# Short MLP of a two-sequence encoder layer: weights loaded raw and split on GpSimd, in place of split copies made in the long down stage

## The reference

```python
def encoder_layer(x, ...):
    ...                                    # RG-LRU branch and attention branch, merged
    x = layer_norm(ALPHA * x + mix, ln1_g, ln1_b)
    hu = depthwise_conv(x @ w_up + b_up, w_ffn_conv, b_ffn_conv, FFN_CONV_PAD)   # w_up: 1024 x 6144
    val, gt = jnp.split(hu, 2, axis=-1)
    ffn = (jax.nn.gelu(gt) * val) @ w_down + b_down                              # w_down: 3072 x 1024
    return layer_norm(ALPHA * x + ffn, ln2_g, ln2_b)

y_prompt = encoder_layer(y_prompt, ...)    # 512 positions
y_sample = encoder_layer(y_sample, ...)    # 1024 positions
```

## Time and profile before

| | |
|---|---|
| median of 3 executions | 2669.51 us (2669.5 to 2674.13) |
| span of the profiled execution | 2675.3 us |
| TensorE busy | 2601.6 us, 97% |
| VectorE busy | 1629.2 us, 61% |
| ScalarE busy | 958.3 us, 36% |
| GpSimd busy | 573.8 us, 21% |

### The profile page before, as it was taken

One profiled execution on the slowest core, in us unless ns is written; L12 is line 12 of the kernel. 1 busy time (PEld: TensorE's weight loads), 2 busy tenths in 40 slices (PEclk: granted clock), 3 DMA queues, 4 the chain that ended last, 5 costly groups with the idle time before them and its releaser, 6 DMA issues.

```text
span 2675.3 us, 32667 instructions
## 1 busy us (share of the span) xinstructions
PE 2601.6 (97%) x11634; PEld 2144.6 (80%) x11634; DVE 1629.2 (61%) x2037; ACT 958.3 (36%) x1346; POOL 573.8 (21%) x306
## 2 busy tenths in 40 slices
PE   8998999999999999899999999999999999999998
PEld 6887888888778878788888888877788777888886
DVE  6899756435703649888888576467642325644445
ACT  3676713213400015444444333358732312111112
POOL 3554532232133522323232022300000000000000
PEclk9999999999999999999999999999999999999999
DMA  5665644544686843444444799976656793555544
GB/s 215 206 197 169 205 177 146 184 158 164 234 344 223 301 170 148 151 179 155 175 158 171 269 384 335 354 244 222 222 189 221 258 355 142 193 193 193 194 190 159
DMA packets 199872, 571.81 MB, mean 214 GB/s; under 512 B 16167, under 2 KB 43047, under 8 KB 197712
## 3 DMA queue, kind: packets, MB, share of 16 engines
q1 hardware_dynamic: 143712, 469.75, 48.7%
q10 hardware_dynamic: 56048, 100.59, 10.6%
HBM read 338.25 MB, written 223.10 MB: 210 GB/s over the span
## 4 chain that ended last, share of the span: by engine, by line
PE 77%; DVE 10%; DMA 7%; ACT 3%; issue 1%; ACTq 0%; SPq 0%; POOL 0%; DVEq 0%; POOLq 0%
PE ps L1182 33%; PE ps L1587 14%; PE ps L1363 8%; PE ps L1537 5%; PE ps L1457 5%; PE ps L1649 4%; DMA gate_in<-gate_dram 3%; PE ps L1226 2%; DMA raw<-w_down 2%; PE ps L1346 2%; PE ps L1396 1%; PE ps L1383 1%; DVE tau L2450 1%; DMA W<-w_split 1%; PE ps L1233 1%
## 5 line engine op out<-in xcount | busy, mean ns | idle before, releaser
L1182 PE MATMUL ps<-XH,W 128*128 128x512 f32 x2752 | 811.8, 393 | 25.6 <-POOL W L1041 10.3
L1182 PEld LDWEIGHTS ps<-XH,W 128*128 128x128 f32 x2752 | 519.4, 189 | 143.7 <-issue 11.9
L1182 PE MATMUL ps<-XL,W 128*128 128x512 f32 x1376 | 483.9, 391 | 0.0
L1182 PEld LDWEIGHTS ps<-XL,W 128*128 128x128 f32 x1376 | 260.2, 189 | 54.1
L1649 PE MATMUL ps<-Wd,Hd 128*128 128x512 f32 x1152 | 262.7, 390 | 2.1 <-DVE Hd L2919 2.0
L1649 PEld LDWEIGHTS ps<-Wd,Hd 128*128 128x128 f32 x1152 | 215.7, 188 | 48.9 <-DVE Hd L2919 3.3
L1363 PE MATMUL ps<-XH,W 128*128 128x512 f32 x672 | 216.4, 393 | 0.0
L1040 POOL TENSOR_SCALAR W<-raw 128x1024 fp32r<-128x1024 f32 (+2 forms) x72 | 88.5, 1230 | 564.1 <-PE ps L1182 295.7
L1041 POOL TENSOR_TENSOR W<-raw,W 128x1024 fp32r<-128x1024 f32 (+2 forms) x72 | 203.4, 2825 | 6.0
L1128 POOL TENSOR_TENSOR A<-raw,A 128x512 fp32r<-128x512 f32 x66 | 127.6, 1934 | 308.9 <-ACT A L2144 302.4
L1587 PE MATMUL ps<-XH,A 128*128 128x512 f32 x528 | 170.1, 390 | 0.0
(11 more groups left out here) (304 smaller groups left out, 4661.3 us busy)
## 6 DMA issues: line engine op xcount, KB each, us to landing
W<-w_split SPq DMA_DIRECT2D x130, 1024.0 KB, 6.8
w_split<-W SPq DMA_DIRECT2D x59, 1024.0 KB, 6.2
w_split<-A SPq DMA_DIRECT2D x66, 512.0 KB, 3.8
raw<-w_up SPq DMA_DIRECT2D x48, 512.0 KB, 5.7
raw<-w_down SPq DMA_DIRECT2D x48, 512.0 KB, 6.4
w_split<-Wd SPq DMA_DIRECT2D x24, 1024.0 KB, 8.4
raw<-w_qkv_mix SPq DMA_DIRECT2D x28, 512.0 KB, 4.0
h_dram<-l_h SPq DMA_DIRECT2D x24, 512.0 KB, 3.8
```

The lines of the kernel that those rows point to most:

```text
L1182: last = nc.tensor.matmul(bank(group, c), lhs(wl, k), rhs(xl, k, c), start=(k == 0 and n == 0), stop=(k == nk - 1 and n == 2))
```

## The change

The long down stage no longer stores its split down slabs, and no longer loads, splits and stores the rest quadrants. All of `save_down`, `load_rest`, `save_rest` and the GpSimd loop over the rest go, with the waits on them.

In the short MLP, a down slab (n = 8 to 11) is loaded raw from `w_down` (512 KB), into the place of the tail of its slot. An even up slab (n = 0, 2, 4, 6) is loaded in two DMAs: columns 512 to 1023 as head and tail from `w_split` (512 KB), and columns 0 to 511 raw from `w_up` (256 KB), again into the place of the tail. Odd up slabs are fetched as before. GpSimd makes the head and then, in place, the tail, slab by slab in the order 0, 2, 4, 6, 8, 9, 10, 11, and TensorE waits for it.

```diff
+        at_short = [at_w + 5120, at_w + 15360]
+            at_short.append(spot[0] + 4096)
+        short_raw = [place(f"short_raw{i}", [P, D_MODEL], at=a) for i, a in enumerate(at_short)]
...
-        rest_raw = [place(f"rest_raw{i}", [P, CH], at=form_at["F0"] + 2048 * i) for i in range(2)]
-        rest = [place(f"rest{i}", [P, 2, CH], F32R, at=form_at[n]) for i, n in enumerate(("F1", "F2"))]
...
-                def save_down(s, slot, slab):
-                    sp.wait_ge(step_split, s + 1)
-                    sp.dma_start(w_split[slab, :, :, 0:D_MODEL], W_down[slot][:, :, :].bitcast(F32)).then_inc(w_saved[slot], 16)
...
-                def load_rest(i, slab, k):
-                    sp.dma_start(rest_raw[k][:, :], A["w_up"][slab, :, 0:CH]).then_inc(rest_in[k][0], 16)
-
-                def save_rest(i, slab, k):
-                    sp.wait_ge(rest_split, i + 1)
-                    sp.dma_start(w_split[slab, :, :, 0:CH], rest[k][:, :, :].bitcast(F32)).then_inc(rest_saved[k][0], 16)
...
-                    if s % 2 == 0:
-                        save_down(s - 2, (s - 2) % RING, down_slab(s - 2))
-                    else:
-                        next_rest((s - RING) // 2)
...
+                def fetch_mlp(free, g, n):
+
+                    slot, slab = SLOT[n], FIRST["mlp"] + 12 * g + n
+                    if n >= 2 * FG:
+                        sp.wait_ge(slab_done, free)
+                        sp.dma_start(short_raw[slot][:, :], A["w_down"][FG * g + n - 2 * FG, :, :]).then_inc(w_landed[slot], 16)
+                    elif n % 2:
+                        fetch(free, slab, slot)
+                    else:
+                        sp.wait_ge(slab_done, free)
+                        sp.dma_start(slabs[1][slot][:, :, CH:D_MODEL].bitcast(F32), w_split[slab, :, :, CH:D_MODEL]).then_inc(w_landed[slot], 16)
+                        sp.dma_start(short_raw[slot][:, 0:CH], A["w_up"][2 * FG * g + n, :, 0:CH]).then_inc(value_landed[n // 2], 16)
...
-                    for i in range(FAST):
-                        k = i % 2
-                        pool.wait_ge(rest_in[k][0], REST_BASE + 16 * (i // 2 + 1))
...
-                        order(pool.tensor_scalar(rest[k][:, 0, :], rest_raw[k][:, :], 1.0, 1.0, ALU.mult, ALU.mult))
-                        pool.tensor_tensor(rest[k][:, 1, :], rest_raw[k][:, :], rest[k][:, 0, :].bitcast(F32),
-                                           ALU.subtract).then_inc(rest_split, 1)
...
+                def split_short(slot, width):
+
+                    head = slabs[1][slot][:, 0, 0:width]
+                    pool.sem_inc(begun, 1)
+                    order(pool.tensor_scalar(head, short_raw[slot][:, 0:width], 1.0, 1.0, ALU.mult, ALU.mult))
+                    pool.tensor_tensor(slabs[1][slot][:, 1, 0:width], short_raw[slot][:, 0:width], head.bitcast(F32),
+                                       ALU.subtract).then_inc(short_split, 1)
+
+                with order.loop(NG, 2 * FG) as g:
+                    for n in range(0, 2 * FG, 2):
+                        pool.wait_ge(value_landed[n // 2], 32 + 16 * g + 16)
+                        split_short(SLOT[n], CH)
+                    for kk in range(FG):
+                        pool.wait_ge(w_landed[DOWN_SLOT[kk]], 16 * use(1, "mlp", 2 * FG + kk, g))
+                        split_short(DOWN_SLOT[kk], D_MODEL)
...
+                    elif phase == "mlp" and n >= 2 * FG:
+                        pe.wait_ge(short_split, 2 * FG * g + n - FG + 1)
                     else:
                         pe.wait_ge(w_landed[slot_of(q, phase, n)], 16 * use(q, phase, n, g))
+                        if phase == "mlp" and n % 2 == 0:
+                            pe.wait_ge(short_split, 2 * FG * g + n // 2 + 1)
...
-                                saves = min(s, FT) // RING if s % 2 == 0 else max(0, s - FT) // RING
-                                act.wait_ge(w_saved[slot], 16 * (TOTAL[0][slot] + saves))
```

More of the change, by code:

```diff
@@ L510, in build @@
         form_saved, FORM_BASE = z_loaded, 16 * (KD // 2)
-        rest_in, REST_BASE = gate_loaded, 16 * KD
-        rest_saved, SAVED_BASE = mix_stored, 16 * KD
         down_rounded = sem("down_rounded")
         step_split = h_split[0]
-        rest_split = sem("rest_split")
+        short_split = sem("short_split")
+        value_landed = [y_in[i][1] for i in range(FG)]
         step_used = sem("step_used")
@@ L928, in _ @@
                     load_h(s, 0, s)
-                    if s == 2:
-                        save_down(0, 0, down_slab(0))
                 def next_step(s, kk, half, k):
@@ L935, in next_step @@
                     load_h(kk, half, k)
[L937 to L942, removed]
                 for s in range(RING, FT):
@@ L949, in _ @@
                         store_h(FT - 1)
-                    if s % 2 == 0:
-                        save_down(s - 2, (s - 2) % RING, down_slab(s - 2))
-                    else:
-                        next_rest((s - RING) // 2)
                 for s in range(FT, STEPS):
                     next_step(s, s - FT, 1, s % RING)
[L956 to L963, removed]
                 sp.wait_ge(plain_saved, 16 * 4 * PLAIN)
-                for k in range(2):
-                    sp.wait_ge(rest_saved[k][0], SAVED_BASE + 8 * FAST)
                 for slot in range(4):
-                    sp.wait_ge(w_saved[slot], 16 * TOTAL[0][slot] + 16 * (FT // RING))
+                    sp.wait_ge(w_saved[slot], 16 * TOTAL[0][slot])
                 sp.wait_ge(wo_saved, 16 * 6)
@@ L1020, in _ @@
                     first_use = SLOT[n] not in SLOT[:n]
-                    fetch(s0 + (2 if first_use and n > 2 else 3 - SLABS["w_o"] if first_use else n - slot_user(n) + 3),
-                          FIRST["mlp"] + n, SLOT[n])
+                    fetch_mlp(s0 + (2 if first_use and n > 2 else 3 - SLABS["w_o"] if first_use else n - slot_user(n) + 3), 0, n)
                 with sp.Fori(0, NG - 1) as i:
                     for n in range(12):
-                        fetch(s0 + 12 * i + n + 12 + 3 - slot_user(n), FIRST["mlp"] + 12 * i + n + 12, SLOT[n])
+                        fetch_mlp(s0 + 12 * i + n + 12 + 3 - slot_user(n), i + 1, n)
             @block.gpsimd
@@ L2339, in _ @@
                         for slot in range(2, 4):
-                            act.wait_ge(w_saved[slot], 16 * TOTAL[0][slot] + 16 * (FT // RING))
+                            act.wait_ge(w_saved[slot], 16 * TOTAL[0][slot])
                     end_phase(act, end_of(q, "mlp"), wait=False)
```

10 lines of the change are left out of this document (removed).

## The result

The changed kernel takes 2681.77 us (median of 4 runs, 2681.34 to 2682.34). The kernel before takes 2669.51 us (2668.54 to 2674.13). The ratio is 1.0046, 95% interval 1.0032 to 1.0061, so the change costs 12.3 us. The prediction was 2672.9 us, "within 0.2%" most likely, with a range up to 2679.5 us. It is wrong on both counts.

What follows compares the result with a forecast made beforehand. TensorE, busy for 97% of the span, was taken to bound the kernel, so only its idle time counted. Terms -2.5 - 0.6 + 0.6 + 3.8 + 1.3 + 0.8 = +3.4 us on 2669.5 gave 2672.9 us, range 2666 to 2679.5.

Steps and rivals of the forecast that it cites:

- Part 1: Long down stage: fewer stores and loads let raw slabs land earlier, ending TensorE's three waits; gain 2.5 us (0 to 2.6).
- the long stage gives nothing: Rival, long down stage: its three waits come from VectorE's order of work, not the DMAs; 2675.4 us, chance 0.07.
- Part 2: Short MLP, slab 7: lands sooner with half-size raw slabs behind it; gain 0.6 us in all (0 to 1.2).
- Part 3: Short MLP, even up slabs: second issue, landing and split fit before need, slab 2 tightest with 2.2 us spare; cost nothing.
- Part 4: Short MLP, slab 8: GpSimd's split is 0.1 us late in each of six groups; cost 0.6 us (0 to 6.6).
- Part 5: Slabs 9 to 11, groups 0 to 4: GpSimd splits faster than TensorE's 5.45 us per slab; cost nothing.
- Part 6: Last group, slabs 8 to 11: GpSimd can't keep up with TensorE and hinders VectorE; cost 3.8 us (1.9 to 6).
- The strict rule: VectorE instructions with two SBUF inputs and GpSimd instructions reading SBUF exclude each other throughout; would make the sum 2.2 us higher.
- taking turns: Rival: GpSimd and VectorE exclude each other wherever they meet; +9.9 us, 2679.4 us, chance 0.23.
- Part 7: Group 0: four GpSimd splits push back VectorE's backlog, delaying its last `HL`; cost 1.3 us (0 to 3.1).
- Part 8: Start of the short MLP: two half tails fall into VectorE's row splitting the normed input; cost 0.8 us (0 to 2).
- The test signs: Profile checks: last down product some 4 us longer, GpSimd splits about 149 us, groups 1 to 4 near 66.2, L2722's mean.

Runs made afterwards that it cites:

- e_same: The kernel before, unchanged, profiled a second time: 2670.15 us against 2670.39, ratio 0.9995.
- e_short_only: The kernel before's long down stage with all its stores, joined to the changed kernel's short MLP: 2683.24 us against 2670.39, ratio 1.0052.
- e_up: The kernel before's long stage, with only the even up slabs raw in the short MLP: 2674.22 us against 2669.21, ratio 1.0020.
- e_down: The kernel before's long stage, with only the down slabs raw in the short MLP: 2676.59 us against 2669.21, ratio 1.0026.
- e_last_four: The changed kernel, with the last group multiplied like the others, all four position tiles slab by slab: 2679.72 us against 2670.39, ratio 1.0038.
- e_after: The changed kernel again, unchanged: 2680.7 us against 2669.44 for the kernel before, ratio 1.0043.
- e_memset: The changed kernel, each GpSimd tail in the short MLP replaced by two write-only instructions: 2670.0 us against 2669.44 for the kernel before, ratio 1.0001.
- e_start: The changed kernel, with slabs 0 and 2 of group 0 fetched whole: 2681.2 us against 2669.21 for the kernel before, ratio 1.0035.
- e_middle: The changed kernel with raw loads and GpSimd splits only in groups 1 to 4: 2667.47 us, ratio 0.9992 to before; repeated, 2667.24 us, 0.9994.

## Why the prediction was wrong

The step that failed is the price of GpSimd's turns with VectorE, in parts 6, 7 and 8. The prediction took 3.8 + 1.3 + 0.8 = 5.9 us for them, because it let VectorE lose only part of what it overlaps; the runs show 4.8 + 4.3 + 2.6 = 11.7 us. Of that, 1.7 us is TensorE at the halved clock behind a wait, for which the sum had no term at all. That the engines take turns was in the prediction, as the upper end and as a rival.

**What bounds the kernel** was read rightly: only TensorE's idle time counted, and the long stage had 2.5 us of it. That what is late ahead of a slab is paid in full also held, at the ends of the short MLP.

**Part 1** was right: -2.5 us forecast. Against e_same the stage is 3.3 us shorter, in every trace that has the new stage. The old stage itself varies: the five traces that have it (the first of before, e_same, e_short_only, e_up, e_down) lie +0.2, 0, +0.1, -1.1 and -2.7 us from e_same, -0.7 in the mean, so the mean gain is 2.6 us. The rival "the long stage gives nothing" falls.

**Part 2** failed, by 0.6 us: slab 7 still takes 5.27 to 5.35 us to land (5.30 to 5.42 in e_same), so smaller slabs behind it make it no faster that could be seen. **Part 3** held, with no wait at slab 2 outside the start. **Part 4** was 0.6 us too high. The split of slab 8 in the last group was ready at 2643.20, 5.2 us after slab 7 began, where the forecast had 5.0 and a need at 5.8 (here 2643.60). It was in time in every group of both traces of the changed kernel (in group 0 of e_last_four TensorE waited 0.32 us for it). **Part 5** held within 0.4 us in all.

**Part 6**, 4.8 us against 3.8 (in e_after and e_down 6.4, with the halved clock). The mechanism was right, and so was its range; the choice in it was 1.0 us too low. I discounted the turns because VectorE waits for ScalarE in part of this time. That saves less than I took off: GpSimd's tail is so long that whatever VectorE starts beside it waits for its end. Slab 11 was ready 17.3 us after slab 7 began (15.9 undisturbed, 20 by my strictest count). The fourth slab had to wait for `HL`, held up by the last tail, 1.0 us longer still.

The strict rule that the prediction set beside its sum (the Trainium skill, "SBUF — State Buffer", section "Who interferes with whom") would have given 6 us here, 3.1 in group 0 and, as the rival *taking turns*, 2679.4 us in all. It was the better guide for the whole, and 1.2 us too high in the last group. The prediction quoted it only for instructions with two inputs. The same section of the Trainium skill also names `cast` and `tensor_scalar` among those that can take the ports that the two engines share, in the modes in which they use two ports, and says that a two-input instruction isn't in the way of a GpSimd instruction that only writes. The traces agree with both: a one-input TENSOR_SCALAR (2.71 us) and a CAST (2.48 us) stood behind GpSimd's tail as long as the others, and in e_memset they waited for a write too, while `HL` didn't.

**Part 7**, 4.3 us against 1.3. The wait itself is 2.35 us, near the upper end (3.1), so the backlog was pushed back nearly as far as counted at most: 12.9 us, where 13.8 us of GpSimd instructions had been counted. That count left out the even up slabs. Without them (e_down) it is pushed back by 9.9 us and the `HL` is just in time, so it was luck that the total came near. The second term, 1.7 us at the halved clock behind the wait, was in no step. Neither term is fixed: group 0 cost 4.3, 4.7 and 4.5 us in the traces of the changed kernel, e_after and e_start, but 1.9 and 2.2 us in e_last_four and e_short_only, where the wait for `HL` was 1.18 and 1.97 us and the clock stayed up.

**Part 8**, 2.6 us against 0.8 (0 to 2). Two instructions of VectorE each stood 1.0 us longer in a row without slack. I had priced this by the mean length of the two half tails, and not by following the hold-up of each short instruction, by a tail three times as long, to the next `x`.

**Sum.** With the measured terms: -2.6 (long stage) + 0 + 0 + 0 + 0.4 + 4.8 + 4.3 + 2.6 = +9.5 us in place of +3.4. The medians say +12.3 and +11.3. The piece of 1.7 us that e_after has and the first trace doesn't would close most of that, but how often such pieces fall into an execution, and whether that is all of the rest, stays open.

**The test signs** did their work: the last down product took 4.8 us more than before, for some 4 forecast, and none of groups 1 to 4 is longer than 66.4 us; GpSimd's splits took 145.4 us (49.1 + 96.3) for 149 forecast, L2722 (now L2701) went from 752 to 955 ns and its neighbour L2724 (now L2703) to 1180, so the turns are real by my own criterion. Of the rivals, *taking turns* had the place and the mechanism, with 2679.4 us still 2.4 us short; it took slab 8 for 2.4 us, which cost nothing, and had no term for the clock. I gave it 0.23, held back by the gaps of VectorE in groups 1 to 4. Those gaps were real and made these groups free; they said nothing about the three places where there are none.

## What to carry to other kernels

A split moved to GpSimd is paid by VectorE: wherever both work out of SBUF, count every VectorE instruction that would begin beside a GpSimd tail as ending after it (33 of 33 here), and follow the delay to the first place without slack. Here GpSimd's work was free in the middle turns of the loop, and not in the first and the last, so look whether the work can be moved in the middle turns alone (e_middle against the changed kernel: 13 to 14 us). And where TensorE is nearly always busy, a new wait of some 2 us can cost nearly as much again in a piece at the lower clock behind it.

## What the runs showed of the hardware

Beside a GpSimd tail of 128x1024 (2.4 us alone, 2.7 beside VectorE), VectorE's 128x512 instructions of one input went from 0.55 to 2.71 us and from 0.43 to 2.48 us, those of two inputs from 0.75 to 2.77 us. The end came 0.28 us (one input) or 0.55 us (two inputs) after the tail's. The additions of 128x1024 that read PSUM (L2724 of the changed kernel, 1.225 us) say nothing about this: none of the 20 ran beside an instruction of GpSimd. Instructions of GpSimd that only write (e_memset) held up no two-input `HL` (0.692 us mean, seven of them begun beside a write). One-input instructions waited for the write to end: casts took 0.71 to 0.73 us in place of 0.43, a TENSOR_SCALAR up to 1.1 us in place of 0.55, again ending 0.28 us behind it.

Of three short waits of TensorE (0.79, 1.00 and 2.19 us) in the last group, none was followed by the halved clock in the first trace. In e_after and e_down a piece of 3.4 us at half the clock followed in the same place, in e_short_only and e_start none. In group 0 it followed the wait of 2.35 and 2.31 us in the two traces of the changed kernel and the 2.56 us wait of e_start, and not the waits of 1.97 us in e_short_only and 1.18 us in e_last_four. At the start of the short MLP, with waits of 0.4 to 1.5 us, such a piece fell in e_up, e_short_only, e_last_four and e_memset, and in neither trace of the changed kernel. What decides this is not settled by these runs.
